# Block 2's feed-forward passes take x unnormed, with the norm's factor put on gate and silu; block 1's attention masks, scales and takes the minimum in one VectorE pass

## The reference, cut to what matters

```python
def dsa_mixer(...):                    # block 1, per head
    s = einsum(q, k_sel) * att_scale
    s = where(valid, s, -inf); p = softmax(s); o = einsum(p, v_sel)

def rmsnorm_2(x, g):
    return x * rsqrt(mean(x * x) + EPS) * g
def modulate(h, shift, scale):
    return h * (1 + scale) + shift
def swiglu(h, w_in, w_out):
    gate, up = split(h @ w_in)         # 2 x 2816 columns
    return (silu(gate) * up) @ w_out

# block 2, at the end of each layer (the context xc only in layer 0)
x  = x  + g2  * swiglu(modulate(rmsnorm_2(x,  norm2_g), sh2,  sc2),  w_ffn_in, w_ffn_out)
xc = xc + cg2 * swiglu(modulate(rmsnorm_2(xc, norm2_g), csh2, csc2), w_ffn_in, w_ffn_out)
```

## Time and profile before

| what | value |
|---|---|
| time, median of 3 runs | 2719.97 us (2719.34 to 2720.1) |
| profiled execution: time / span | 2719.45 us / 2717.6 us |
| TensorE busy | 2638.6 us, 97% of the span |
| VectorE busy | 1906.1 us, 70% |
| ScalarE busy | 1327.2 us, 49% |
| GpSimd busy | 428.4 us, 16% |
| mean granted TensorE clock | 0.991 |

### The profile page before, as it was taken

One profiled execution on the slowest core, in us unless ns is written; L12 is line 12 of the kernel. 1 busy time (PEld: TensorE's weight loads), 2 busy tenths in 40 slices (PEclk: granted clock), 3 DMA queues, 4 the chain that ended last, 5 costly groups with the idle time before them and its releaser, 6 DMA issues.

```text
span 2717.6 us, 40457 instructions
## 1 busy us (share of the span) xinstructions
PE 2638.6 (97%) x17090; PEld 2297.3 (85%) x17090; DVE 1906.1 (70%) x2548; ACT 1327.2 (49%) x1674; POOL 428.4 (16%) x344
## 2 busy tenths in 40 slices
PE   8999998999999999999999999999999999899998
PEld 7889787888889877888898777778888899789887
DVE  8857476785876657687699655457777779765774
ACT  6445445444544545544523655624444443776443
POOL 3410010331330001033005211010000003321000
PEclk9999999999999999999999999999999999999999
DMA  7556694555555688356333321235555544434653
GB/s 246 189 187 183 218 295 143 182 183 195 187 185 180 194 259 268 125 187 205 89 94 98 92 75 63 63 125 186 185 193 192 177 120 129 117 113 148 209 178 101
DMA packets 442330, 445.57 MB, mean 164 GB/s; under 512 B 13711, under 2 KB 433672, under 8 KB 442150
## 3 DMA queue, kind: packets, MB, share of 16 engines
q1 hardware_dynamic: 438744, 436.80, 50.2%
q0 software_dynamic: 2400, 5.40, 0.9%
q10 hardware_dynamic: 1006, 0.79, 0.1%
HBM read 441.79 MB, written 1.17 MB: 163 GB/s over the span
## 4 chain that ended last, share of the span: by engine, by line
PE 82%; DVE 8%; ACT 6%; issue 3%; DMA 1%; POOL 1%; POOLq 0%; SPq 0%; ACTq 0%; DVEq 0%
PE bank L1849 30%; PE bank L1809 19%; PE bank L1853 16%; PE bank L1801 6%; PE bank L1844 3%; PE bank L2116 2%; DVE R L3091 1%; DVE lower L765 1%; DVE lower L2497 1%; PE bank L2350 1%; ACT lower L1126 1%; PE bank L2038 1%; PE bank L2341 1%; PE bank L2205 1%; PE bank L2125 1%
## 5 line engine op out<-in xcount | busy, mean ns | idle before, releaser
L2497 DVE TENSOR_TENSOR lower<-ring,upper 128x2048 fp32r<-128x2048 f32 (+1 forms) x238 | 567.9, 2388 | 270.4 <-ACT upper L1172 270.2
L1172 ACT ACTIVATE upper<-ring 128x2048 fp32r<-128x2048 f32 (+1 forms) x238 | 441.7, 1863 | 452.6 <-PE bank L1853 449.5
L1849 PE MATMUL bank<-h_pair,upper 128*128 128x512 f32 x2464 | 606.4, 393 | 17.8 <-DVE h_pair L2550 8.3
L1849 PEld LDWEIGHTS bank<-h_pair,upper 128*128 128x128 f32 x2464 | 455.6, 189 | 110.1 <-issue 17.5
L1809 PE MATMUL bank<-h_up,lower 128*128 128x512 f32 (+1 forms) x1280 | 338.5, 347 | 3.6 <-DVE R L2693 1.8
L1853 PE MATMUL bank<-h_pair,lower 128*128 128x256 f32 x2464 | 339.3, 284 | 0.0
L1853 PEld LDWEIGHTS bank<-h_pair,lower 128*128 128x128 f32 x2464 | 325.0, 192 | 11.3
L1849 PE MATMUL bank<-hid_pair,upper 128*128 128x512 f32 x1232 | 297.4, 392 | 0.0
L1809 PEld LDWEIGHTS bank<-h_up,lower 128*128 128x128 f32 x1280 | 223.7, 189 | 51.2 <-issue 19.0
L1849 PEld LDWEIGHTS bank<-hid_pair,upper 128*128 128x128 f32 x1232 | 225.7, 188 | 43.2
L765 DVE TENSOR_TENSOR lower<-ring,lower 128x2048 fp32r<-128x2048 f32 x70 | 166.7, 2381 | 121.5 <-ACT lower L1126 121.4
(11 more groups left out here) (363 smaller groups left out, 4377.9 us busy)
## 6 DMA issues: line engine op xcount, KB each, us to landing
ring<-in_w_ffn_in SPq DMA_DIRECT2D x154, 1024.0 KB, 5.1
ring<-in_w_ffn_out SPq DMA_DIRECT2D x56, 1024.0 KB, 4.9
ring<-in_w_mix_in SPq DMA_DIRECT2D x48, 1024.0 KB, 5.4
ring<-in_w_mod SPq DMA_DIRECT2D x48, 1024.0 KB, 5.8
ring<-in_w_in SPq DMA_DIRECT2D x42, 1024.0 KB, 5.3
ring<-in_w_ffn_out SPq DMA_DIRECT2D x28, 768.0 KB, 4.2
ring<-in_w_mix_out SPq DMA_DIRECT2D x16, 1024.0 KB, 5.5
ring<-in_w_in SPq DMA_DIRECT2D x16, 512.0 KB, 5.0
```

What stands on the lines that cost most here:

```text
L1172: act.activation(f.upper(p)[:, 0:n], slot[:, 0:n], ACT.Copy).then_inc(up_ready, 1)
L1849: pe.matmul(bank[:, 0:2 * T], up[:, cols], x_pair.rearrange("p e t -> p (e t)"), start=first, stop=False)
L2497: dve.tensor_tensor(f.lower(p)[:, 0:n], slot[:, 0:n], f.upper(p)[:, 0:n].bitcast(F32), ALU.subtract)\
```

## The change

In block 2's passes the reciprocal is no longer taken ahead of the split. With s the root and r = 1/s, the pass is now given h' = x * gain + shift * s, which is s times the old h. ScalarE forms x * gain ahead of the root, between its squares (`gained_h`; 8 instructions of 128x256 for each half); behind the root VectorE forms shift * s + that (`whole_part`), ScalarE copies it to the upper part, VectorE subtracts (`low_part`, now a plain subtraction). The reciprocal of the root is taken in the pass itself, when the first piece is empty and before the `split_low` of piece 3, and GpSimd's `scale_pass` now runs in block 2's three passes too: r on the gate, r on the silu. With it the order of the queues inside block 2's passes becomes that of block 1's. The last pair of squares at the entry is cut in two, each waiting for its own half of the last residual (`first_half_added`, `first_sq_ready`). The three sums of squares in GpSimd's queue for block 1 are the same as before, called from another place.

In block 1's attention one VectorE instruction per key group computes (scores + mask) * (-scale) and its minimum; two of them take the place of one addition, two maxima and one multiplication. The exponential now has scale -1. TensorE's wait for the bank of unit i-2 moves from the masked scores to the same instruction's minimum (`nmx_ready`).

```diff
-            def squares(n, nh, x_done, f=None, half=0):
+            def gained_h(gain, half, chunks):
+                for c in chunks:
+                    act.activation(x_gained[half][:, c, :], xT[:, half, c, :], ACT.Identity, scale=gain(c, half))\
+                       .then_inc(h_gained, 1)
+
+            def ffn_squares(n, x_done, f, gain, layer):
                 root_table()
                 for i in range(4):
-                    if f and i == 3:
+                    if i == 3:
                         split_up(f, 0)
-                    x_done(i)
-                    act.activation(squares_of(nh)[:, :, 2 * i:2 * i + 2, :], xT[:, half:half + nh, 2 * i:2 * i + 2, :],
-                                   ACT.Square).then_inc(sq_ready, 1)
+                        act.wait_ge(first_half_added, layer + 1)
+                        act.activation(squares_of(1)[:, 0, 6, :], xT[:, 0, 6, :], ACT.Square).then_inc(first_sq_ready, 1)
+                        x_done(3)
+                        act.activation(squares_of(1)[:, 0, 7, :], xT[:, 0, 7, :], ACT.Square).then_inc(sq_ready, 1)
+                    else:
+                        x_done(i)
+                        act.activation(squares_of(1)[:, :, 2 * i:2 * i + 2, :], xT[:, 0:1, 2 * i:2 * i + 2, :],
+                                       ACT.Square).then_inc(sq_ready, 1)
+                    gained_h(gain, 0, (2 * i, 2 * i + 1))
                 norm_root(n, root[:, 0:T])
...
-                    act.activation(h_up[:, c, :], h_whole[:, c, :], ACT.Identity, bias=shift(c)).then_inc(h_up_ready, 1)
+                    act.activation(h_up[:, c, :], h_whole[:, c, :], ACT.Copy).then_inc(h_up_ready, 1)
...
                     filled(act, it)
-                    if p % 2 == 0 and not f.gain:
-                        evicted(act, it)
-                        act.activation(glu[q % 3], glu[q % 3], ACT.Silu).then_inc(silu_ready, 1)
                     split_up(f, p + NUP)
...
-                    if p % 2 == 1 and f.gain:
+                    if p % 2 == 1:
                         act.wait_ge(gate_scaled, f.hidden(q))
                         act.activation(glu[q % 3], glu[q % 3], ACT.Silu).then_inc(silu_ready, 1)
-                    if f.gain and p % 2 == 0 and q:
+                    elif q:
                         hidden_up(f, q - 1)
-                    if p % 2 == 1 and not f.gain:
-                        hidden_up(f, q)
...
                 if layer == 0:
                     for half in range(2):
+                        scale_pass(ffn2[half])
                         add_squares(3 * DEPTH + 3 + half, 3 * DEPTH + half)
+                else:
+                    scale_pass(ffn2[2])
...
-            def plain_h(f, norm_n, gain, chain, half, shift):
-                norm_factor(norm_n, chain, root[:, 0:T])
-                chain.settle()
+            def shifted_h(f, norm_n, shift):
+                dve.wait_ge(root_ready, norm_n + 1)
                 for c in range(KD):
-                    whole_part(c, gain, half)
+                    whole_part(f, c, shift, 0)
...
-                dve.scalar_tensor_tensor(out=h_whole[:, c, :], in0=xT[:, half, c, :], scalar=gain(c, half),
-                                         in1=root[:, 0:T], op0=ALU.mult, op1=ALU.mult).then_inc(h_whole_ready, 1)
+                dve.wait_ge(h_gained, (f.n - 2 * DEPTH) * KD + c + 1)
+                dve.scalar_tensor_tensor(out=h_whole[:, c, :], in0=root[:, 0:T], scalar=shift(c),
+                                         in1=x_gained[half][:, c, :], op0=ALU.mult, op1=ALU.add)\
+                   .then_inc(h_whole_ready, 1)
...
-                dve.scalar_tensor_tensor(out=h_low[:, c, :], in0=h_whole[:, c, :], scalar=shift(c),
-                                         in1=h_up[:, c, :].bitcast(F32), op0=ALU.add, op1=ALU.subtract)\
+                dve.tensor_tensor(h_low[:, c, :], h_whole[:, c, :], h_up[:, c, :].bitcast(F32), ALU.subtract)\
                    .then_inc(h_ready, 1)
...
-                    if f.gain:
+                    if p == 0 and f.gain:
                         split_low(f, p + NUP)
-                    if p == 0 and f.gain:
                         dve.wait_ge(root_ready, f.norm + 1)
                         dve.reciprocal(root[:, 0:T], root[:, 0:T]).then_inc(r_ready, 1)
-                    if f.gain and p % 2 == 0 and q:
+                    elif p == 0:
+                        dve.reciprocal(root[:, 0:T], root[:, 0:T]).then_inc(r_ready, 1)
+                        split_low(f, p + NUP)
+                    else:
+                        split_low(f, p + NUP)
+                    if p % 2 == 0 and q:
                         hidden_low(f, q - 1)
                     if p % 2 == 1:
-                        dve.wait_ge(glu_scaled if f.gain else silu_ready,
-                                    f.hidden(q))
+                        dve.wait_ge(glu_scaled, f.hidden(q))
...
-            def mask_unit(u0, i, chain):
+            def mask_unit(u0, i):
...
-                dve.tensor_tensor(buf[:, 0:UNIT_W], M[i % 2][:, 0:UNIT_W], selb, ALU.add).then_inc(s_masked, 1)
-                dve.wait_ge(s_masked, u0 + i + 1)
                 for r, keys in enumerate(UNIT_KEYS):
-                    chain(dve.tensor_reduce(mx[:, b, r:r + 1], buf[:, keys].rearrange("p (r j) -> p r j", r=1), AX.X,
-                                            ALU.max))
-                chain.settle()
-                dve.tensor_scalar(nmx[:, b, :], mx[:, b, :], -ATT_SCALE, None, ALU.mult).then_inc(nmx_ready, 1)
+                    ins = dve.tensor_tensor_reduce(buf[:, keys], M[i % 2][:, keys], selb[:, keys], -ATT_SCALE, 3e38,
+                                                   ALU.add, ALU.min, nmx[:, b, r:r + 1])
+                ins.then_inc(nmx_ready, 1)
...
                 def second_half(at):
-                    if at == 3:
-                        norm_factor(n_norm, chain, root[:, 0:T])
-                        chain.settle()
+                    if at == 4:
+                        dve.wait_ge(root_ready, n_norm + 1)
                     if at in (4, 7):
                         for c in range(0, 4) if at == 4 else range(4, KD):
-                            whole_part(c, modded(32), 1)
+                            whole_part(ffn2[1], c, shifts[1], 1)
```

More of the change, by code:

```diff
@@ L649, in program @@
         branch_up_ready, branch_split = sem("branch_up_ready"), sem("branch_split")
+        x_gained = [R[:, 0:KD * T].rearrange("p (c t) -> p c t", c=KD), h_whole]
+        h_gained, first_half_added, first_sq_ready = (sem(n) for n in ("h_gained", "first_half_added", "first_sq_ready"))
         up2_ready, low2_ready = sem("up2_ready"), sem("low2_ready")
@@ L1200, in hidden_up, with ffn @@
                 act.activation(hid_of(hid_up, q), hid_of(hid_whole, q), ACT.Copy).then_inc(hid_up_ready, 1)
-            def ffn(f, shift=None, ahead=None):
+            def ffn(f, ahead=None):
                 if not f.gain and not f.prepared:
-                    ffn_h(f, shift, range(KD))
+                    ffn_h(f, range(KD))
                     for p in range(1, NUP):
@@ L1691, in _ @@
                 f = ffn2[2 * layer]
-                shifts = [lambda c, layer=layer, half=half: mod[:, layer, 24 + c, half:half + 1] for half in range(2)]
-                squares(n_norm, 1, item_done(f.item - 4), f, 0)
+                ffn_gain = lambda c, half, layer=layer: mod[:, layer, 32 + c, half:half + 1]
+                ffn_squares(n_norm, item_done(f.item - 4), f, ffn_gain, layer)
                 n_norm += 1
@@ L1699, in second_half @@
                         plain_squares(1)
+                    elif at in (2, 4):
+                        gained_h(ffn_gain, 1, range(0, 4) if at == 2 else range(4, KD))
                     elif at == 3:
@@ L1702, in second_half @@
                     elif at in (5, 8):
-                        ffn_h(ffn2[1], shifts[1], range(0, 4) if at == 5 else range(4, KD))
+                        ffn_h(ffn2[1], range(0, 4) if at == 5 else range(4, KD))
                 def next_layer(at):
@@ L1712, in next_layer @@
                         half_up(1, 0, h2_early, 1, range(0, 4) if at == 5 else range(4, KD))
-                ffn(f, shifts[0], None if last else second_half)
+                ffn(f, None if last else second_half)
                 if not last:
                     n_norm += 1
-                    ffn(ffn2[1], None, next_layer)
+                    ffn(ffn2[1], next_layer)
                 pos += len(layer2_pieces(item, layer)[0])
@@ L1770, in pooled_sums, with sum_squares @@
                 mm.then_inc(ssq_filled, 1)
-            def sum_squares(n, nh):
+            def sum_squares(n, nh, by_chunk=None):
                 for c in range(KD):
-                    if c % 2 == 0:
+                    if c == KD - 2 and by_chunk:
+                        pe.wait_ge(first_sq_ready, by_chunk)
+                    elif c % 2 == 0 or by_chunk and c == KD - 1:
```

(17 more changed lines are left out.)

35 lines of the change are left out of this document (15 added, 20 removed).

## The result

The changed kernel takes 2704.51 us (median of 4 runs, 2702.48 to 2708.45) against 2719.65 for the kernel before (2718.66 to 2720.1): ratio 0.9943, interval 0.9931 to 0.9956, 15.1 us faster. The forecast was 2711.3, 8.7 us faster, with a range that ended at 2706. The direction was right; the gain is 1.7 times the forecast's. A later set of 5 runs of the same kernel gave 2705.21, ratio 0.995 (0.9937 to 0.9962).

A forecast was written before the change was run, and what follows sets the result against it. TensorE, busy 97% of the span, was taken as the bound, so only its waits could give time. Entries 4.36, attention 2.6 and clock 1.76 made 8.7 us, forecast 2711.3, range 2706 to 2716.5.

The forecast's parts named there:

- Entries, waits: Entries of ffn2[0] and ffn2[2]: reciprocal off the path, 1.79 us each, plus 0.39 us each later; together 4.36 us.
- the fourth piece: Behind the first chunks of block 2's entry: TensorE's wait of 0.39 us taken as gone, 0.78 for two.
- gained_h: Eight ScalarE instructions ahead of the root, 4.0 us, claimed hidden by waits; uncovered they would cost 1.0 us per entry.
- the last squares: Sum of squares at the entry: it ran without a pause, so cutting them in two gives nothing by itself.
- ffn2[1]: Second half's pass: its reciprocal moves to the first in piece, nothing gained or lost, 0.
- GpSimd's passes: Block 2's in pieces: two GpSimd multiplications for each of 33 pairs, as in block 1, cost 0.
- the rival of a slower VectorE: Block 2's in pieces: GpSimd slows VectorE's splits, up to 34 us, 2745 with the gains; chance 0.07.
- Attention, waits: Block 1's attention: a unit falls from 1.35 to 0.92 us, three per layer on the path, 2.6 us saved.
- The rival that priced it at 0.199: Attention: accumulator read priced as ScalarE's, attention gives 1.1 us, clock stays down, 2714.5; chance 0.10.
- Clock: Products behind `mod_rows` fast again, 0.88 us twice, 1.76 (bounds 0 and 2.8); entries counted 0.
- the forecast's best case: Sums up to 14 us: clock back at an entry as well, attention at its best; 2706.
- Theory C: Set up for the follow-ups: beside shorter waits, TensorE's clock stays up behind them, worth as much again.

The follow-up runs named there:

- ffn_fill: Changed kernel with the old attention, plus 4 idle products at each of the two entries of block 2's passes: 2711.1 us, ratio 0.9973.
- att_longer: Changed kernel with one more unread VectorE instruction of 128x180 ahead of each attention unit's two: 2707.42 us, ratio 0.9957.
- before_fill_att: Kernel before, with 16 and 15 idle transposes in TensorE's attention waits for `mod_rows` and the second last head's outputs: 2719.92 us, ratio 1.0002.
- before_fill_entry: Kernel before, with eight idle products behind each sum of squares at the entries: 2720.85 us, ratio 1.0007.
- after_fill: Changed kernel with idle products or transposes in TensorE's waits at entries, `mod_rows`, second last head's outputs and indexer: 2700.07 us, ratio 0.993.
- best: Changed kernel with idle products at entries, `mod_rows` and indexer, and the mixer's seventh lower part moved behind the last head's: 2695.82 us, ratio 0.9917.

## Why the prediction came out low

**Entries, waits: right.** The reciprocal left the path (wait 4.15 to 2.30, 1.85 where 1.79 was forecast). At the fourth piece the starts moved by 0.65, not 0.39; the wait of 0.39 is gone, and the rest shows at the first products behind it, with no row that explains it. Together 2.5 per entry, 5.0 against 4.36. `gained_h`, the last squares, `ffn2[1]` and GpSimd's passes cost nothing, as forecast, and the rival of a slower VectorE didn't come: its split runs at 3.32 beside GpSimd as in block 1. The Trainium skill's "SBUF — State Buffer", section "Who interferes with whom", names the pair that contends; the trace agrees also for `hid_low` (1.79 beside GpSimd, 0.68 without).

**Attention, waits: right mechanism, mis-sized term.** The forecast's term was 3 units x 2 layers x 0.43 = 2.6, from a unit of 0.92 between the bounds 0.68 and 1.16. The unit takes 0.63, so 0.72 is saved, and 6 x 0.72 = 4.3; the trace shows 4.4. That the two agree is partly luck: the two units ahead of `mod_rows` gave 0.97 per layer and not 1.44, so that the wait there is 2.06 and not 1.81, and behind it 1.20 came where one unit, 0.72, was counted, at two waits for a weight piece's lower part. The new instructions run like plain passes (0.28 and 0.42), and what I took for dear, the read of the accumulator, is 0.084 and starts together with the next instruction (both at 418.74), not ScalarE's 0.199. By the Trainium skill's rule ("VectorE: DVE Perf Modes", "Two Vector instructions with no wait between them") such an op is two instructions: the trace agrees, with 32 rows of the read. The rival that priced it at 0.199 falls.

**Clock: the step that failed.** The prediction said "At the entries 4.15 - 1.79 = 2.36 us stays above 2.22, so the clock still falls there and I count 0". It didn't fall at either entry of the changed kernel's two profiles, and at idle of 2.30 us it falls in fewer than half the cases. A single row (2.22, drop) was read as a border, where rows at equal idle go either way. The row without a drop (1.84) is no border either: at the same wait, 1.78 us in `ffn_fill`, the clock fell:

```profile
2218.36 0.36 PE L1825 MATMUL bank<-h_up,lower 128*128 128x256 f32 x1 [1.78 <-DVE R L2709]
```

```profile
2218.40:2221.60 3.20, 3.20 (x18) 3.20 (x19) 3.20 (x9) 0.53 (x2) 0.00 (x0) 0.63 0.88 300
```

And the attention's 1.76 (bound: 2.8) counted only the eight products behind one wait, while slow products go on behind them, and the second drop of layer 0, behind `ya_pair`, stood in no term: the two attentions gave 8.7 - 4.4 = 4.3 us beyond the waits, the entries 7.9 - 5.0 = 2.9. That is in one pair of profiles; of the medians' 15.1 us, 15.1 - 9.4 = 5.7 remain for it, where 1.76 was forecast. This remainder was not measured by itself. Of the 6.4 us beyond the forecast, 3.9 are thus this step's, 1.8 the unit's price and 0.6 the fourth piece's; neither of the first two alone gives the 14 us of the forecast's best case.

**Is it the clock?** That a kept clock is time in the changed kernel is shown: holding the clock alone gives 4.4 us (3.1 of it, by the trace, at the indexer, which the change doesn't touch), and lengthening the entry's wait costs the wait and as much again. Theory C in its plain form fell, though: in the kernel before a kept clock at the entries is worth nothing, because VectorE and ScalarE set the fourth piece, and behind `mod_rows` VectorE takes part of it back. The clock's part is a gain of two edits together, the shorter wait behind which the clock falls less often, and the earlier VectorE which lets TensorE use it. For the attention, the kept clock is shown in traces (1.1 us lost in `att_longer`, 1.5 and 1.6 won in `before_fill_att`) and not in a median by itself; at the entries `ffn_fill` has it in the trace and not in the median.

How the 5.7 divide between the two is not shown. The mean granted clock that each run lists gives an estimate: it is 0.9914 over 60 runs of the kernel before and 0.9940 over nine of the changed kernel, and runs of the kernel before at 0.994 take 4.3 us less than those at 0.989, about 0.85 us per 0.001. By that price the difference of 0.0026 is worth 2.2 us. The rest would be time for which TensorE waits on VectorE in the kernel before when its clock stays up (1.47 and 1.51 us in place of 0.39 at the fourth pieces of `before_fill_entry`, 0.84 and 0.85 behind `mod_rows`) and which the new orders remove.

## What to carry to other kernels

On an engine that is busy 97% of the span, a wait costs its length and often as much again in slower products behind it; read the granted clock behind every wait before a change, and ask next whether another engine would hide the faster products. One row with a drop and one without don't make a border: take several executions, and give such a term a chance and both ends. When a fused instruction replaces several passes, price it first at its plain passes over the same data.

## What was not expected of the hardware

VectorE's read of its accumulator shows as a row of its own, 0.081 to 0.085 us, less than half of ScalarE's 0.199. Idle transposes of the identity into a free bank held TensorE's clock: with 20 of them in 2.35 us, in a wait of 3.31, the clock over 10 us behind it was 1.00 where it is 0.83 in the changed kernel. In the 12 profiles without these transposes the clock fell at both waits of the indexer, in the two with them (`after_fill`, `best`) at neither. Timeline and window of `after_fill`, then the window of the changed kernel:

```profile
279.97 2.35 PE L2163 MATMUL bank<-ident 128*128 128x128 f32 x20
283.45 0.49 PE L2170 MATMUL bank<-R 64*128 64x128 f32 x4 [1.13 <-ACT R L1425]
```

```profile
283.40:293.40 10.00, 9.95 (x104) 8.08 (x108) 4.40 (x7) 4.54 (x11) 0.00 (x0) 1.00 0.66 216
```

```profile
283.50:293.50 10.00, 9.93 (x87) 7.37 (x88) 4.40 (x7) 3.92 (x10) 0.00 (x0) 0.83 0.67 213
```
